# A decoder trunk in which two of the mixer's small matmul groups change places with a projection

## The chip, the cores and the metric

The kernel runs on one NeuronCore of a Trainium2 chip. The metric is the time of one execution on the device, in microseconds; lower is better.

## The reference, cut to what matters

Two layers (DEPTH = 2), each of a half-step SwiGLU, a mixer, a cross attention to a memory, and a second half-step SwiGLU, every one with a residual and a layer norm; 512 positions by 1024 features, float32. The change touches only the mixer:

```
xa, ya, q, k, v, g, lr, c = split_cols(x @ w_in)
# group A, 384 channels in 6 blocks of 64
xc = causal_dwconv(xa, conv_w, conv_b)
r = sigmoid(einsum(xc, w_r) + b_r);  i = sigmoid(einsum(xc, w_i) + b_i)     # recurrent gates
a = exp(-8 * r * softplus(-lam));    h = scan(a, sqrt(1 - a^2) * (i * xc));  out_a = h * gelu(ya)
# group B, 4 heads: gated linear attention in chunks of 64
log_alpha = log_sigmoid(lr @ w_gate + b_gate) / 16                           # linear gates
o = gla_chunked(q, k, v, log_alpha)
o = o * rsqrt(mean(square(o)) + EPS) * norm_g * silu(g)                      # heads' mean squares
# group C, 256 channels in 4 groups of 64
u = causal_dwconv(a_c * sigmoid(gate_c), dw_w, dw_b)                         # 31 taps
out_c = silu((u - mu) * rsqrt(var + EPS) * gn_g + gn_b)                      # group norm
y = concatenate([out_a, out_b, out_c]) @ w_out
```

## The kernel before, in words

Activations lie as features by positions: a tile is 128 features by 512 positions. Each weight and each activation is split into a rounded high part and a low rest, and a product is three passes: high by high, high weight by low activation, low weight by high activation. `tile_of` (line 853) makes one such output tile from 8 feature tiles: 16 passes with the high weights (lines 862 and 865), then 8 with the low ones (line 868), 24 passes in all. `MIX_STEPS` gives each projection of the mixer its PSUM bank and the read that must have freed that bank (`BANK_FREE`).

The weights of a tile are a "slot". Four slots are held as loaded (`raw`), two as split. ScalarE makes the high part of a slot (`w_hi_of`, line 1568) and GpSimd the low part (line 740). `step(layer, s)` in ScalarE's program makes the high part of slot s + 2, after TensorE has finished with slot s. ScalarE's `read(kind, i)` in the mixer is that step followed by the bank, so that every copy out of a projection's bank stands behind making the high weights of the second projection after it. In the mixer the slots come in the order xa 0 to 2, cg 0, ca 0, k 0, k 1, q 0, q 1, cg 1, ca 1, v (two slots), g 0 to 2, ya 0 to 2, then the memory's keys.

The order of the work on each engine is written out by hand; semaphores tie the engines. TensorE's order in the mixer is the list that the change edits. Small matmuls in plain float32 stand between the projections:

- `recurrent_gates(t)`: two 128x512 matmuls (line 1225) for channels tile t, into banks 4 to 7; it waits for the short convolution, and for t = 2 for ScalarE's reads of the first pair.
- `linear_gates()`: two 64-row matmuls (line 1232), into banks 6 and 7; it waits for the copy of k 0 and for the second pair's reads.
- `group_norm(0, SQ, ...)`: one 128x512 matmul (line 1323), the variance of the first group-norm tile.
- `mean_squares()`: three 128x512 matmuls (line 1316) into bank 4, the heads' mean squares.

The profile shows each of these plain float32 matmuls as two records.

ScalarE's order around the first place (lines 1943 to 1978), which the change does not touch:

```
rg_sigmoids(0); rg_sigmoids(1)                       # line 1896, two ACTIVATEs each
A(KK[0], read("k", 0), ACT.Copy)                     # makes q 0's high weights, then copies k 0
rg_sigmoids(2)                                       # waits for the third pair of gates
... 3 Tanh, 3 Exp on the recurrent gates             # lines 1953, 1955
A(KK[1], read("k", 1), ACT.Copy)                     # makes q 1's high weights, then copies k 1
... the linear gates: Abs, Identity, Exp, Ln         # lines 1960 to 1967
A(QQ[0], read("q", 0), ACT.Copy)                     # makes cg 1's high weights, then copies q 0
... 3 Sqrt, decay exponentials; between them read("q", 1)   # makes ca 1's high weights
```

Around the second place ScalarE does: gelu of ya 0, squares of the three head outputs, gelu of ya 1 (behind the step for the first key slot), `group_root(0)` (line 1918, waits for the variance), `head_root()` (line 1908, waits for the mean squares), gelu of ya 2. VectorE's decays (line 2606) wait for the linear gates' logarithm from ScalarE, and its conv taps (line 2585) fill the time between.

Of the kernel before, what the change touches and what calls it, by code (L numbers as in the profile page):

```python
# [163 lines left out]
def raw_norm(layer, n):  # L164
    return layer * len(RAW_NORMS) + RAW_NORMS.index(n)
# [125 lines left out]
def hybrid_decoder(nc, x_in, mem_in, consts_in, vecs_in, mats_in, w_in1, w_out1, w_in2, w_out2,  # L291
                   w_mix, w_v, w_mixout, w_kv, w_q, w_o, out):
    ctx = ExitStack()
    with ctx:
# [85 lines left out]
        def bank(b, rows=P, cols=SEQ):  # L380
            return psum[0:rows, b, 0:cols]
# [30 lines left out]
        def tiles_of(n, count):  # L412
# [37 lines left out]
                                                                 k=KT // 2)  # L450
# [384 lines left out]
        def _(pe):  # L835
# [17 lines left out]
            def tile_of(layer, s, o, operand, n, start=True, stop=True, hi_arrived=None,  # L853
                        lo_arrived=None):
                r = ring(layer, s)
                hi_ready(layer, s)
                for k in range(n):
                    hi = weight(r, k)[0]
                    b_hi, b_lo = operand(k)
                    if hi_arrived:  # L860
                        hi_arrived(k)
                    nc.tensor.matmul(o, hi, b_hi, start=start and k == 0, stop=False)  # L862
                    if lo_arrived:
                        lo_arrived(k)
                    nc.tensor.matmul(o, hi, b_lo, start=False, stop=False)  # L865
                slot_ready(layer, s)
                for k in range(n):
                    last = nc.tensor.matmul(o, weight(r, k)[1], operand(k)[0],  # L868
                                            start=False, stop=stop and k == n - 1)
                last.then_inc(slot_multiplied, 1)  # L870
# [329 lines left out]
            def mixer(layer):  # L1200
                E = layer * EVACS

                def project(kind, i):
                    free = BANK_FREE[kind, i]
                    if free:
                        pe.wait_ge(evac, E + EV[free])
                    if (kind, i) == ("ca", 0):
                        pe.wait_ge(raw_sums_read, 2 * raw_norm(layer, 0) + 2)
                    if (kind, i) == ("ca", 1):
                        pe.wait_ge(xc_ready, layer * AT + AT)  # L1210
                    if (kind, i) == ("k", 0):
                        pe.wait_ge(x_returned, 2 * layer + 1)
                    tile_of(layer, S_MIX + MIX_SLOT[kind, i], bank(MIX_BANK[kind, i]),
                            normed if (kind, i) == ("ca", 0) else act, KT)
# [4 lines left out]
                def recurrent_gates(t):  # L1219
                    pe.wait_ge(xc_ready, layer * AT + t + 1)  # L1220
                    for g in range(2):
                        n = 2 * t + g
                        if n >= 4:
                            pe.wait_ge(rg_gate_read, layer * 6 + n - 3)
                        nc.tensor.matmul(bank(4 + n % 4), mats[:, (AT * g + t) * P:][:, 0:P],
                                         XC[t], start=True, stop=True).then_inc(rg_gate_ready, 1)

                def linear_gates():
                    pe.wait_ge(evac, E + EV["k", 0])
                    pe.wait_ge(rg_gate_read, layer * 6 + 4)  # L1230
                    for g in range(2):
                        last = nc.tensor.matmul(
                            bank(6 + g), mats[0:CHUNK, (2 * AT + g) * P:][:, 0:P],
                            KK[0][0:CHUNK, :], start=True, stop=True)
                    last.then_inc(gla_gate_ready, 1)
# [53 lines left out]
                def output(j):  # L1289

                    if j == 0:
                        pe.wait_ge(state_ready, layer * (NCHUNK - 1) + NCHUNK - 1)
                    for t in range(TT):
                        cols = slice(t * P, (t + 1) * P)
                        for h in range(HEADS):
                            e = h * DV + j * 32
                            nc.tensor.matmul(psum[h * 32:(h + 1) * 32, 5 + j, cols],
                                             v_tok[:, t, e:e + 32], SC[h][:, cols],
                                             start=True, stop=False)
                        for n in (2 * t, 2 * t + 1):  # L1300
                            if n:
                                cols = slice(n * CHUNK, (n + 1) * CHUNK)
                                for h in range(HEADS):
                                    g, r0 = h // 2, h % 2 * CHUNK
                                    last = nc.tensor.matmul(
                                        psum[h * 32:(h + 1) * 32, 5 + j, cols],
                                        state[r0:r0 + CHUNK, n - 1, g, j * 32:(j + 1) * 32],
                                        QQ[g][r0:r0 + CHUNK, cols],
                                        start=False, stop=n % 2 == 1)
                    last.then_inc(o_ready, 1)  # L1310

                def mean_squares():
                    pe.wait_ge(block32_set, 1)
                    for j in range(DVT):
                        pe.wait_ge(o_read, layer * DVT + j + 1)
                        last = nc.tensor.matmul(bank(4), block32[:, :], OSQ[j], start=j == 0,
                                                stop=j == DVT - 1)
                    last.then_inc(rms_ready, 1)

                def group_norm(t, source, ready, signal):  # L1320

                    pe.wait_ge(ready, layer * CT + t + 1)
                    nc.tensor.matmul(bank(CONV_BANK[t]), block64, source[t],
                                     start=True, stop=True).then_inc(signal, 1)
# [18 lines left out]
                recurrent_gates(0)  # L1343
                recurrent_gates(1)
                project("k", 0)
                recurrent_gates(2)
                project("k", 1)
                linear_gates()
                project("q", 0)
                project("q", 1)  # L1350
# [14 lines left out]
                project("ya", 0)  # L1365
                for j in range(DVT):
                    output(j)
                group_norm(0, SQ, gn_squared, gn_var)
                project("ya", 1)
                mean_squares()  # L1370
                project("ya", 2)
                memory_key(0)
# [168 lines left out]
            for layer in range(0, LAYERS):  # L1541
                ffn(layer, 0, 0)
                mixer(layer)
                attention(layer)
                ffn(layer, 1, 3)
# [1396 lines left out]
```

## Time and profile before

| | |
|---|---|
| median of 3 runs | 2122.47 us (2122.47 to 2122.51) |
| profiled execution, its own time | 2121.4 us |
| its span | 2119.6 us |
| TensorE busy | 2099.8 us, 99% |
| VectorE / ScalarE / GpSimd busy | 72% / 51% / 35% |
| mean granted TensorE clock | 0.998 |

The span is what the profile's rows cover; the execution's own time has 1.8 us more around it. "Idle before" in a row is how long that engine had been idle ahead of the row, and the name behind it is what released it. Rows of one kind that touch are merged, with their count behind the x. The mixer runs once in each layer; the stretch that the change touches begins near 385 us and again near 1435 us.

### The profile page before, as it was taken

How to read it: one execution, taken by the hardware profiler on the slowest of the kernel's cores; microseconds unless marked ns; L12 is line 12 of the kernel's file. 1: busy time of each engine (PE TensorE's matmuls, PEld its weight loads, DVE VectorE, ACT ScalarE, POOL GpSimd, SP SyncE). 2: the span in 40 equal slices, each digit the busy share in tenths (PEclk: the TensorE clock that was granted, in tenths of full speed). 3: DMA queues.
4: the chain of work that ended last, by engine and by line, in shares of the span. 5: the costliest groups of instructions: out<-in, count | busy, mean ns of one | idle time of the engine just before them, and what ended most of it. 6: DMA issues, size and time to landing. Idle time of an engine off the chain costs nothing.

```text
span 2119.6 us, 33832 instructions
## 1 busy us (share of the span) xinstructions
PE 2099.8 (99%) x13480; PEld 1882.2 (89%) x13480; DVE 1519.7 (72%) x1965; ACT 1083.5 (51%) x1631; POOL 746.1 (35%) x353
## 2 busy tenths in 40 slices
PE   9999999999999999999999999999999999999997
PEld 7999989788888999998889998897787889999986
DVE  5888535987756998863498884369878479888534
ACT  3666524836344556652366664257364445666422
POOL 4100344536563520024350003445266535100343
PEclk9999999999999999999999999999999999999999
DMA  4555522333332355552245555223243223555531
GB/s 171 139 163 161 185 96 62 90 104 104 113 98 70 106 154 155 165 183 96 77 140 151 159 154 180 92 70 90 90 119 122 88 68 122 150 153 166 172 102 44
DMA packets 118973, 260.99 MB, mean 123 GB/s; under 512 B 41888, under 2 KB 54560, under 8 KB 118560
## 3 DMA queue, kind: packets, MB, share of 16 engines
q1 hardware_dynamic: 109008, 241.95, 35.1%
q0 software_dynamic: 9216, 16.78, 5.3%
q8 instruction: 108, 1.77, 0.3%
q14 instruction: 49, 0.40, 0.1%
q10 hardware_dynamic: 592, 0.08, 0.0%
HBM read 250.38 MB, written 8.39 MB: 122 GB/s over the span
## 4 chain that ended last, share of the span: by engine, by line
PE 95%; ACT 2%; DVE 1%; POOL 1%; issue 0%; DVEq 0%; DMA 0%; ACTq 0%; SPq 0%
PE psum L868 15%; PE psum L862 15%; PE psum L865 15%; PE psum L1059 11%; PE psum L1061 11%; PE psum L1063 11%; PE psum L880 2%; PE psum L1020 1%; PE psum L962 1%; PE psum L1160 1%; PE psum L1159 1%; PE psum L964 1%; PE psum L967 1%; PE psum L886 1%; PE psum L1165 1%; PE psum L837 1%
## 5 line engine op out<-in xcount | busy, mean ns | idle before, releaser
L740 POOL TENSOR_TENSOR w_lo<-raw,w_hi 128x1024 fp32r<-128x1024 f32 (+2 forms) x222 | 611.5, 2758 | 776.6 <-ACT w_hi L1568 755.2
L1568 ACT ACTIVATE w_hi<-raw 128x1024 fp32r<-128x1024 f32 (+2 forms) x222 | 257.3, 1159 | 592.8 <-PE psum L868 514.5
L2398 DVE TENSOR_TENSOR w_lo<-raw,w_hi 128x1024 fp32r<-128x1024 f32 (+2 forms) x204 | 249.9, 1225 | 49.2 <-ACT w_hi L1736 49.1
L1736 ACT ACTIVATE w_hi<-raw 128x1024 fp32r<-128x1024 f32 (+2 forms) x204 | 215.0, 1056 | 108.0 <-PE psum L1063 62.7
L791 POOL DMA_DIRECT2D raw<-w_in x64 | 55.5, 867 | 568.9 <-DMA raw<-w_in 568.8
L862 PE MATMUL psum<-acts_hi,w_hi 128*128 128x512 f32 x632 | 251.2, 397 | 0.0
L865 PE MATMUL psum<-acts_lo,w_hi 128*128 128x512 f32 x632 | 246.2, 390 | 0.0
L865 PE MATMUL psum<-h_lo,w_hi 128*128 128x512 f32 x616 | 239.7, 389 | 0.0
L862 PE MATMUL psum<-h_hi,w_hi 128*128 128x512 f32 x616 | 239.7, 389 | 0.0
L2186 DVE SCALAR_TENSOR_TENSOR x<-x,psum 128x512 f32<-128x512 f32 x54 | 37.0, 685 | 249.3 <-PE psum L868 249.3
L1063 PE MATMUL psum<-acts_hi,w_lo 128*128 128x256 f32 x688 | 194.7, 283 | 0.0
L1061 PE MATMUL psum<-acts_lo,w_hi 128*128 128x256 f32 x688 | 194.7, 283 | 0.0
L1059 PE MATMUL psum<-acts_hi,w_hi 128*128 128x256 f32 x688 | 194.7, 283 | 0.0
L1748 ACT ACTIVATE work<-psum 128x256 f32<-128x256 f32 x272 | 104.4, 384 | 102.6 <-PE psum L1063 96.2
L868 PE MATMUL psum<-acts_hi,w_lo 128*128 128x512 f32 x632 | 156.1, 389 | 0.0
L1059 PE MATMUL psum<-t_in_x,w_hi 128*128 128x256 f32 x544 | 154.4, 284 | 0.0
L1063 PE MATMUL psum<-t_in_x,w_lo 128*128 128x256 f32 x544 | 153.9, 283 | 0.0
L1061 PE MATMUL psum<-t_in_x,w_hi 128*128 128x256 f32 x544 | 153.9, 283 | 0.0
L868 PE MATMUL psum<-h_hi,w_lo 128*128 128x512 f32 x616 | 148.7, 389 | 0.0
L2198 DVE TENSOR_TENSOR work<-work 128x512 f32<-128x512 f32 x52 | 137.3, 2640 | 14.3 <-ACT work L1600 12.5
L862 PEld LDWEIGHTS psum<-acts_hi,w_hi 128*128 128x128 f32 x632 | 118.7, 188 | 28.3 <-issue 3.9
L865 PEld LDWEIGHTS psum<-acts_lo,w_hi 128*128 128x128 f32 x632 | 118.7, 188 | 26.3 <-issue 2.4
(396 smaller groups left out, 5453.2 us busy)
## 6 DMA issues: line engine op xcount, KB each, us to landing
raw<-w_in SPq DMA_DIRECT2D x176, 512.0 KB, 3.6
raw<-w_out SPq DMA_DIRECT2D x64, 704.0 KB, 4.2
raw<-w_in SPq DMA_DIRECT2D x64, 256.0 KB, 3.9
raw<-w_in POOLq DMA_DIRECT2D x64, 256.0 KB, 4.1
raw<-w_kv SPq DMA_DIRECT2D x32, 512.0 KB, 3.4
raw<-w_mix SPq DMA_DIRECT2D x26, 512.0 KB, 3.5
raw<-w_q SPq DMA_DIRECT2D x16, 512.0 KB, 3.4
raw<-w_o SPq DMA_DIRECT2D x16, 512.0 KB, 3.5
```

The source lines that it names most:

```text
L740: nc.gpsimd.tensor_tensor(w_lo[:, n % SPLIT, 0:width], raw[:, n % RAW, 0:width], w_hi[:, n % SPLIT, 0:width].bitcast(F32), ALU.subtract).t ...
L862: nc.tensor.matmul(o, hi, b_hi, start=start and k == 0, stop=False)
L865: nc.tensor.matmul(o, hi, b_lo, start=False, stop=False)
L868: last = nc.tensor.matmul(o, weight(r, k)[1], operand(k)[0], start=False, stop=stop and k == n - 1)
L1059: nc.tensor.matmul(o, hi[:, cols], x_hi[:, k, :], start=start and k == 0, stop=False, skip_group_check=True)
L1061: nc.tensor.matmul(o, hi[:, cols], x_lo[:, k, :], start=False, stop=False, skip_group_check=True)
L1063: last = nc.tensor.matmul(o, lo[:, cols], x_hi[:, k, :], start=False, stop=k == KT // 2 - 1, skip_group_check=True)
L1568: A(w_hi[:, n % SPLIT, 0:width], raw[:, n % RAW, 0:width], ACT.Copy).then_inc(w_hi_made, 1)
L1736: A(o, source, ACT.Copy).then_inc(unit_hi_made, 1)
L1748: A(kept(name), source, ACT.Copy).then_inc(product_kept, 1)
L2198: V.tensor_tensor(zsqsum, zsqsum, zsq(m), ALU.add).then_inc(z_summed, 1)
L2398: V.tensor_tensor(o, source, hi.bitcast(F32), ALU.subtract).then_inc(unit_split, 1)
```

## The change

In both layers, in TensorE's program alone, the third pair of recurrent gates goes from before projection k 1 to behind it, directly ahead of the linear gates; and the first group norm's variance goes from before projection ya 1 to behind it, directly ahead of the mean squares. No operation is added or removed, and no other engine's program is edited.

```
                 recurrent_gates(0)
                 recurrent_gates(1)
                 project("k", 0)
+                project("k", 1)
                 recurrent_gates(2)
-                project("k", 1)
                 linear_gates()
                 project("q", 0)
...
                 for j in range(DVT):
                     output(j)
+                project("ya", 1)
                 group_norm(0, SQ, gn_squared, gn_var)
-                project("ya", 1)
                 mean_squares()
                 project("ya", 2)
```

## Rows read from the trace of the kernel before

**Rows 1.** The page's first part: busy us, share of the span, instructions.
```profile
PE 2099.8 (99%) x13480; PEld 1882.2 (89%) x13480; DVE 1519.7 (72%) x1965; ACT 1083.5 (51%) x1631; POOL 746.1 (35%) x353
```
**Rows 2.** The page's fourth part: the chain that ended last, by engine.
```profile
PE 95%; ACT 2%; DVE 1%; POOL 1%; issue 0%; DVEq 0%; DMA 0%; ACTq 0%; SPq 0%
```
**Rows 3.** Timeline, TensorE, first layer, the gates: start us, us, what, [idle before].
```profile
385.56 3.60 PE L1225 MATMUL psum<-tmp,mats 128*128 128x512 f32 x8
...
394.46 1.88 PE L1225 MATMUL psum<-tmp,mats 128*128 128x512 f32 x4
...
403.66 0.50 PE L862 MATMUL psum<-acts_hi,w_hi 128*128 128x512 f32 x1
404.00 0.40 PE L865 MATMUL psum<-acts_lo,w_hi 128*128 128x512 f32 x1
```
**Rows 4.** Timeline, TensorE, first passes of q 1, cg 1 and ca 1.
```profile
409.23 0.39 PE L862 MATMUL psum<-acts_hi,w_hi 128*128 128x512 f32 x1
...
414.67 0.39 PE L862 MATMUL psum<-acts_hi,w_hi 128*128 128x512 f32 x1
...
420.11 0.39 PE L862 MATMUL psum<-acts_hi,w_hi 128*128 128x512 f32 x1
```
**Rows 5.** Timeline, ScalarE, first layer, from the second pair's sigmoids to v.
```profile
389.20 0.69 ACT L1896 ACTIVATE tmp<-psum,vecs 128x512 f32<-128x512 f32 x1 [0.17 <-PE psum L1225]
394.66 1.06 ACT L1568 ACTIVATE w_hi<-raw 128x1024 fp32r<-128x1024 f32 x1 [4.77 <-PE psum L868]
...
396.10 1.26 ACT L1896 ACTIVATE tmp<-psum,vecs 128x512 f32<-128x512 f32 x2
...
402.55 1.04 ACT L1568 ACTIVATE w_hi<-raw 128x1024 fp32r<-128x1024 f32 x1
403.50 0.58 ACT L1956 ACTIVATE tmp<-psum 128x512 f32<-128x512 f32 x1
...
410.94 0.58 ACT L1968 ACTIVATE tmp<-psum 128x512 f32<-128x512 f32 x1
...
418.26 1.08 ACT L1568 ACTIVATE w_hi<-raw 128x1024 fp32r<-128x1024 f32 x1
...
425.75 1.49 ACT L1568 ACTIVATE w_hi<-raw 128x1536 fp32r<-128x1536 f32 x1 [2.04 <-PE psum L868]
```
**Rows 6.** ScalarE in one stretch: us, busy us, instructions, clock, DMA share, GB/s.
```profile
401.50:419.90 18.40, 18.21 (x28) 1.00 0.32 78
```
**Rows 7.** Timeline, VectorE: first decay, and the second mask with idle before it.
```profile
409.94 0.69 DVE L2606 SCALAR_TENSOR_TENSOR psum<-psum,tmp 128x512 f32<-128x512 f32 x1
...
456.68 1.37 DVE L2640 COPY_PREDICATED work<-consts,psum 128x1024 f32<-128x1024 uint32 x1 [2.71 <-PE psum L1264]
```
**Rows 8.** Timelines, memory keys: ScalarE's high weights and the TensorE pass they release.
```profile
509.62 1.04 ACT L1568 ACTIVATE w_hi<-raw 128x1024 fp32r<-128x1024 f32 x1
...
510.81 0.35 PE L862 MATMUL psum<-mem_hi,w_hi 128*128 128x256 f32 x1 [0.83 <-ACT w_hi L1568]
```
**Rows 9.** Timelines, second layer: ca 1's high weights and its first pass.
```profile
1468.52 1.08 ACT L1568 ACTIVATE w_hi<-raw 128x1024 fp32r<-128x1024 f32 x1
...
1470.38 0.39 PE L862 MATMUL psum<-acts_hi,w_hi 128*128 128x512 f32 x1
```
**Rows 10.** Timelines, second place: TensorE's variance and mean squares, ScalarE's two roots.
```profile
479.26 1.13 PE L1323 MATMUL psum<-tmp,consts 128*128 128x512 f32 x2
...
485.68 2.74 PE L1316 MATMUL psum<-tmp,block 128*128 128x512 f32 x6
...
488.74 0.69 ACT L1918 ACTIVATE tmp<-psum,small 128x512 f32<-128x512 f32 x1
...
490.03 0.67 ACT L1908 ACTIVATE tmp<-psum,small 128x512 f32<-128x512 f32 x1
```
**Rows 11.** End of the span: us, busy us and count of PE, PEld, DVE, ACT, POOL, clock.
```profile
2100.00:2110.00 10.00, 7.92 (x58) 7.06 (x56) 7.70 (x15) 3.95 (x10) 0.49 (x1) 1.00 0.15 54
2110.00:2119.00 9.00, 0.00 (x0) 0.00 (x0) 6.02 (x12) 4.48 (x9) 4.33 (x5) 0.63 0.50 176
```

More of the change, by code:

```diff
@@ L1345, in mixer @@
                 project("k", 0)
+                project("k", 1)
                 recurrent_gates(2)
-                project("k", 1)
                 linear_gates()
@@ L1367, in mixer @@
                     output(j)
+                project("ya", 1)
                 group_norm(0, SQ, gn_squared, gn_var)
-                project("ya", 1)
                 mean_squares()
```

## The prediction

> **What bounds the kernel now.** I read the page's busy shares first. TensorE is busy 99% of the span, ScalarE about half [rows 1], and the chain that ended last lies on TensorE for 95% [rows 2]. So a small gain can only come from fewer or cheaper TensorE records, and the change has the same records. A loss, though, can come from anything that makes TensorE wait, and that is to be looked for in the engines' orders, not in the shares. The second view is therefore the timeline of TensorE and of ScalarE side by side at the two places. The reader is to see that between the third pair's sigmoids (396.10) and the high weights of ca 1 (418.26) ScalarE stands still nowhere worth naming: in 401.50 to 419.90 it is busy 18.21 of 18.40 us [rows 5, 6]. Here ScalarE is nearly as tight as TensorE, though its share over the span is 51%.
>
> **First place: the third pair behind k 1.** A projection takes 5.44 us, the distance of the first passes of q 1, cg 1 and ca 1 [rows 4] (24 passes of 0.227). On TensorE the swap changes little. The four records of the pair cost about 0.43 each (8 records of the first two pairs in 3.60, the last of them 0.59 long [rows 3]) wherever they stand. What joining them to the linear gates can save is between nothing and all that they cost over ordinary passes, 4 x (0.43 - 0.227) = 0.8 us in a layer; a loss has a reason only if the linear gates' change to 64 rows costs more behind slow records than behind quick ones, and I bound that by the same 0.8. I take 0: whatever it is, it lies ahead of the waits below, which swallow it.
>
> ScalarE's order isn't edited, and it works strictly down its list, as the front part shows: the third pair's sigmoids, three Tanh, three Exp, then q 1's high weights and the copy of k 1. The swap gives it the third pair one projection later. The sum:
> - TensorE's row of the pair begins at 394.46 + 5.44 = 399.90 and ends 1.88 later, 401.78 [rows 3].
> - For the second pair the row ended at 385.56 + 3.60 = 389.16 and the last sigmoid began at 389.20, 0.04 later, and took 0.69 [rows 3, 5]. So the third pair's last sigmoid ends at 401.78 + 0.04 + 0.69 = 402.51.
> - Before, the two ended at 396.10 + 1.26 = 397.36 [rows 5]. ScalarE is 5.15 us late. Ahead of the pair it just idles.
> - Behind it nothing gives the time back until it next waits for TensorE, which is at 425.75, with 2.04 idle [rows 5].
>
> Queued behind the late sigmoids, each by 5.15 us, are what TensorE waits for:
> - q 1: k 1's copy (it frees the bank) ends at 403.50 + 0.58 + 5.15 = 409.23. A pass starts 0.15 after ScalarE ends (509.62 + 1.04 = 510.66, pass at 510.81) [rows 8]. So q 1 starts at 409.38 where it stood at 409.23 [rows 4, 5]. After such a wait the second pass comes 0.34 behind the first (403.66, 404.00 [rows 3]) where 0.227 is usual, 0.11 more. About 0.26 late.
> - cg 1: q 0's copy ends at 410.94 + 0.58 + 5.15 = 416.67, the pass starts at 416.82 where it stood at 414.67: with the 0.11, 2.26 late in all, so a new wait of about 2.0.
> - ca 1: its high weights end at 418.26 + 1.08 + 5.15 = 424.49, the first pass starts at 424.64 where it stood at 420.11: 4.53 + 0.11 = 4.64 late in all, a second wait of about 2.4.
>
> The last of them sets the cost: 4.64 us. The high weights of ca 1 had been 0.77 ahead of their pass, and 5.15 - 0.77 + 0.15 + 0.11 is the same number. Next is v, whose high weights for the second slot wait for TensorE itself, with 2.04 idle before them: from there ScalarE follows TensorE again.
>
> VectorE: its first decay starts at 409.94 [rows 7] behind the linear gates' logarithms, which now come 5.15 later, so it is at most 5.15 late, 0.5 more than TensorE. It has 2.71 idle before the second mask, where it waits for TensorE; I count nothing. GpSimd makes ca 1's low weights from the high ones; TensorE wants them 16 passes, 3.6 us, after its first. Counted as nothing; if both engines' contention for it gave half a microsecond, it would still be covered. The weights' DMAs are issued in an order that stays, and TensorE being late only makes them earlier.
>
> Second layer: ca 1's high weights end at 1469.60 and its pass stands at 1470.38, 0.78 apart [rows 9], against 0.77. Same cost. Together 2 x 4.64 = 9.3 us.
>
> **Second place: the variance behind ya 1.** It takes two records from 479.26 and puts them ahead of the six from 485.68 [rows 10]. The eight still end at 485.68 + 2.74 = 488.42, and ya 1 ends some 0.86 us sooner. ScalarE's first root (488.74) follows gelu of ya 1 and so could start at 487.88; the variance is there by about 484.82 + 1.13 = 485.95. Its second root (490.03) could start at 489.17, 0.75 behind the mean squares. So neither wait bites. What the join saves is between 0 and the excess of two records, 0.4 us in a layer, what it could lose no more; without a row for it I take 0, the nearest, since all eight stay slow. If the cover were gone, the 1.9 us of the first root would be the margin.
>
> **Sum.** Profiled execution 2121.4 + 9.3 = 2130.7. The median of the runs, 2122.47, stands 1.07 above that execution; I put the same 9.3 on it: 2131.7 us. The span would be 2128.9.
>
> **The clock.** The granted clock was 1.00 in 2100 to 2110, with TensorE idle for 2.08 of it, and 0.63 on average in 2110 to 2119, in which TensorE did nothing more [rows 11]. The new waits, 2.0 and 2.4 us, are shorter than that tail, about the size of the idle time that left the clock alone. The Trainium skill ("TensorE: Matmul & The Clock Gate", "HAM oscillation — how this bites in real kernels") has it that an array left idle for long enough falls to half its clock and starts its next work cold; by it two long waits close together are what to be afraid of here. It makes no term of the sum and stands among the rivals.
>
> **Rivals.**
> - *No change.* ScalarE has idle time elsewhere (4.77 before 394.66, 2.04 before 425.75), and 51% says slack. If the delay were taken up before ca 1, the time would be 2122.4, within a few tenths for the saved transitions (at best 2 x (0.8 + 0.4) = 2.4 less, 2120.1). It decides for this case if the delay is under 0.6 us (0.77 less the hand-over). Against it: the idle stretches lie ahead of the late sigmoids and behind ca 1; none between. 6%.
> - *More than this.* A clock drop after the long waits. At 1.2 GHz in place of 2.4 the tile behind it takes up to 5.44 more; once in a layer gives 2131.7 + 10.9 = 2142.6. For it: two waits of over 2 us within 8. Against it: rows 11's first. 4%.
> - *Part of it.* The last wait is smaller, because something in ScalarE's chain that I count as work is itself waiting and shrinks when late. All of what isn't busy in the stretch is 0.19 us in 18.40 [rows 6], so little is there; half of the delay gone would be 2127.1. 4%.
>
> **The numbers.** My forecast 85%, faster by over 0.2% 1%. What a measurement of this kernel can tell from no change is about 0.2%, 4.2 us. Slower by over that needs the forecast or the two last rivals: 0.93; within it 0.06. Range 2128.5 to 2134.0: downwards 1.6 us a layer for savings and a hand-over that I took wrong, upwards some 1.2 a layer for VectorE's half microsecond and GpSimd's.
>
> **What would show it.** In the profile after: the third pair's sigmoids at about 401 to 402.5 with ScalarE idle before them; a TensorE wait released by ScalarE ahead of q 1 (small), cg 1 (about 2.0) and ca 1 (about 2.4), in both layers; v some 4.6 later; the first layer's end later by that and no more; the roots of the second place where they are relative to ya 1. I am wrong if ScalarE's line from Tanh to ca 1 shortens, if ca 1 stands less than 4 us or more than 5.5 later, or if the granted clock falls under 1 in the mixer.

## The result: 9.2 us slower, and the profile after

The changed kernel took 2131.74 us in the median of 6 runs (2131.29 to 2132.24), the kernel before 2122.49 (2122.47 to 2122.67, 6 runs): ratio 1.0045, 95% interval 1.0033 to 1.0056. Forecast was 2131.7, range 2128.5 to 2134.0.

The shares of the page of the profile say nothing of it. Its first part after, against [rows 1]:
```profile
PE 2102.8 (99%) x13480; PEld 1882.7 (88%) x13480; DVE 1520.0 (71%) x1965; ACT 1083.1 (51%) x1631; POOL 744.0 (35%) x353
```
The waits of TensorE over the whole execution say most of it (engine and line, released by what: us in total, times, longest):
```profile
PE psum L862 <- ACT w_hi L1568: 6.0, 4, 2.2
PE psum L862 <- ACT tmp L1968: 3.3, 2, 1.7
```
Before, the first of these was 1.7 us in 2 waits and the second was not there, so 4.3 + 3.3 = 7.6 us of waiting are new. The rest of the loss does not show as idle time: a pass that had to wait starts later than the row's idle time says, by the end of the pass before it (modelled ends overlap the next start by some 0.16 us), and the pass behind it follows 0.1 later than usual.

ScalarE's timeline after, in the first layer, which answers to [rows 5] (start us, us, what, idle before). All of this execution is 0.88 us late here already, before its first pair of gates:
```profile
390.08 0.69 ACT L1896 ACTIVATE tmp<-psum,vecs 128x512 f32<-128x512 f32 x1 [0.17 <-PE psum L1225]
395.53 1.06 ACT L1568 ACTIVATE w_hi<-raw 128x1024 fp32r<-128x1024 f32 x1 [4.76 <-PE psum L868]
...
401.84 0.69 ACT L1896 ACTIVATE tmp<-psum,vecs 128x512 f32<-128x512 f32 x1 [4.77 <-PE psum L1225]
402.70 0.69 ACT L1896 ACTIVATE tmp<-psum,vecs 128x512 f32<-128x512 f32 x1 [0.17 <-PE psum L1225]
...
416.95 0.57 ACT L1968 ACTIVATE tmp<-psum 128x512 f32<-128x512 f32 x1
...
424.27 1.08 ACT L1568 ACTIVATE w_hi<-raw 128x1024 fp32r<-128x1024 f32 x1
```
The reader is to see the new 4.77 us of idle time ahead of the third pair's sigmoids, which is ScalarE waiting for TensorE, and no idle time printed between them and ca 1's high weights (424.27). TensorE after, in the first layer, against [rows 3, 4]:
```profile
386.44 3.60 PE L1225 MATMUL psum<-tmp,mats 128*128 128x512 f32 x8
...
400.78 1.88 PE L1225 MATMUL psum<-tmp,mats 128*128 128x512 f32 x4
402.59 1.98 PE L1232 MATMUL psum<-tmp,mats 64*128 64x512 f32 x4
...
410.15 0.50 PE L862 MATMUL psum<-acts_hi,w_hi 128*128 128x512 f32 x1
...
417.58 0.50 PE L862 MATMUL psum<-acts_hi,w_hi 128*128 128x512 f32 x1 [1.65 <-ACT tmp L1968]
...
425.49 0.47 PE L862 MATMUL psum<-acts_hi,w_hi 128*128 128x512 f32 x1 [2.13 <-ACT w_hi L1568]
```
These are q 1, cg 1 and ca 1, each the first pass behind ScalarE's late work.

The table sets each kernel's TensorE records against the same records of the kernel before: how much later a record starts, in us. Every experiment below is read from it, since it separates the two layers and shows by itself, in its first column, what differs from one execution to the next at the start. From left to right: the first pair of gates in layer 1, then q 1, cg 1, ca 1 and v there, the end of the mixer there, the first pair of gates in layer 2, cg 1 and v there, the last matmul of all. For q 1, cg 1 and ca 1 the record is one a few passes behind the first, so that the slow first pass after a wait is in it. What a layer costs is v less the column at which the layer begins.

| profiled execution of | before 1st pair | q 1 | cg 1 | ca 1 | v | 1st mixer's end | before 2nd | cg 1 | v | last matmul |
|---|---|---|---|---|---|---|---|---|---|---|
| changed | 0.88 | 1.06 | 3.03 | 5.47 | 5.49 | 5.50 | 5.49 | 7.65 | 10.11 | 10.01 |
| e1 first edit only | 1.31 | 1.49 | 3.44 | 5.89 | 5.92 | 5.91 | 5.82 | 8.00 | 10.41 | 10.37 |
| e2 second edit only | 1.02 | 1.02 | 1.02 | 1.02 | 1.02 | 0.99 | 0.99 | 0.99 | 0.99 | 0.91 |
| e3 ScalarE late | 1.13 | 1.58 | 3.55 | 6.00 | 7.66 | 7.63 | 7.60 | 10.06 | 12.52 | 12.43 |
| e5 one Tanh more | 0.00 | 0.00 | 0.00 | 0.23 | 0.26 | 0.23 | 0.45 | 0.45 | 0.68 | 0.57 |
| e6 k 1 first | 0.00 | -0.05 | 1.00 | 3.45 | 3.48 | 3.44 | 3.34 | 4.35 | 8.42 | 8.29 |
| e7 k 1 and q 1 first | 1.31 | 1.27 | 2.31 | 2.33 | 2.33 | 2.29 | 2.25 | 3.26 | 3.26 | 3.25 |
| e4 repaired | 1.45 | 1.40 | 1.40 | 1.40 | 1.97 | 7.95 | 7.86 | 7.82 | 8.41 | 13.37 |
| e9 repaired, taps moved | 1.65 | 1.60 | 1.60 | 1.60 | 2.19 | 2.15 | 2.08 | 2.03 | 2.59 | 2.50 |

In the changed kernel a layer costs 5.49 - 0.88 = 4.61 and 10.11 - 5.49 = 4.62.

The second place after, against [rows 10] (TensorE, then ScalarE):
```profile
490.33 1.02 PE L1323 MATMUL psum<-tmp,consts 128*128 128x512 f32 x2
491.19 2.74 PE L1316 MATMUL psum<-tmp,block 128*128 128x512 f32 x6
```
```profile
493.38 0.69 ACT L1918 ACTIVATE tmp<-psum,small 128x512 f32<-128x512 f32 x1
494.14 0.63 ACT L1920 ACTIVATE tmp<-tmp 128x512 f32<-128x512 f32 x1
494.68 0.67 ACT L1908 ACTIVATE tmp<-psum,small 128x512 f32<-128x512 f32 x1
```
Less the 5.50 of this stretch the mean squares stand at 485.69 (485.68 before) and the roots (lines 1918 and 1908) at 487.88 and 489.18, 0.86 and 0.85 sooner than before: ya 1 ended that much sooner, and no root waits.

### The profile page after: what moved, and what is told of

Same layout as the page of the kernel before. It is cut to its first block, busy times and chain, and to the rows that moved or that the text cites. A ratio compares the mean times of both kernels' runs of the same rounds, so it can differ in the third digit from the quotient of the medians.

```text
span 2129.5 us, 33832 instructions
## 1 busy us (share of the span) xinstructions
PE 2102.8 (99%) x13480; PEld 1882.7 (88%) x13480; DVE 1520.0 (71%) x1965; ACT 1083.1 (51%) x1631; POOL 744.0 (35%) x353
## 4 chain that ended last, share of the span: by engine, by line
PE 93%; ACT 3%; DVE 1%; POOL 1%; issue 1%; DVEq 0%; ACTq 0%; DMA 0%; SPq 0%
PE psum L868 14%; PE psum L862 14%; PE psum L865 14%; PE psum L1059 11%; PE psum L1061 11%; PE psum L1063 11%; PE psum L880 2%; PE psum L1020 1%; PE psum L962 1%; PE psum L1160 1%; PE psum L1159 1%; PE psum L964 1%; PE psum L967 1%; PE psum L886 1%; PE psum L1165 1%; ACT w_hi L1568 1%
```

## The experiments

My theory: the first edit makes ScalarE get its third pair late, its list runs strictly in order, and TensorE waits for what stands behind. The rivals: TensorE itself pays for the joined slow records; the second edit shares in it; VectorE, late as well, sets the end. In the changed kernel's own profile the new waits of TensorE all have ScalarE as their releaser; its waits for VectorE in the mixer are as they were (one of 0.3 us in a layer).

**e1, the first edit alone.**
```
                 project("k", 0)
+                project("k", 1)
                 recurrent_gates(2)
-                project("k", 1)
```


> Only the first edit: the third pair of recurrent gates behind k 1; the variance stays ahead of ya 1. Theory (ScalarE in order): this edit carries all of the loss, 4.62 us a layer in the trace of the changed kernel, so 2131.7 us, with new TensorE waits of 1.7 and 2.1 us ahead of cg 1 and ca 1. Rival (the loss is shared with the second edit, by the eight slow records joined or by the later root): under 2130.

Measured: 2131.54 us (2130.14 to 2133.17) against 2122.12 for the kernel before on that chip, ratio 1.0046 (1.0033 to 1.006). That is all of the loss, to within the interval, and in the table a layer costs 5.92 - 1.31 = 4.61 and 10.41 - 5.82 = 4.59, as in the changed kernel.

**e2, the second edit alone.**
```
+                project("ya", 1)
                 group_norm(0, SQ, gn_squared, gn_var)
-                project("ya", 1)
```


> Only the second edit: the variance behind ya 1, beside the mean squares. Theory: no wait bites, the join of slow records saves at most hundredths: 2122.4 to 2122.5 us, v and everything before as in the kernel before. Rival (the later variance holds up ScalarE's root and what follows): 2123 or more, with ScalarE idle before its line of the first root.

Measured: 2121.92 against 2122.12, ratio 0.9999 (0.999 to 1.0008). In the table its row stays flat. ya 1 itself runs 0.86 sooner (0.16 late where what is around it is 1.02 late), and behind the mean squares all of that but 0.03 is given back. Joining the variance to the mean squares is worth 0.02 to 0.03 us in this layer and nothing that the table shows in the other.

**e3, ScalarE late by other means, TensorE's order as before.** This is the experiment that separates ScalarE's lateness from where the gates stand.
```
                 for t in range(AT):
                     A(TH[t], RR[t], ACT.Tanh, scale=l(11)[:, t:t + 1])
+                for n in range(8):
+                    if n % AT == 0:
+                        act.drain()
+                    A(TH[n % AT], RR[n % AT], ACT.Tanh, scale=l(11)[:, n % AT:n % AT + 1])
```


> The kernel before, with TensorE's order as it was; ScalarE repeats 8 of its Tanh instructions (with 3 drains) behind the third pair's sigmoids, same results. At 0.62 us each that makes it 4.9 to 5.5 us late there. Theory (ScalarE being late is enough by itself): a delay d costs TensorE d - 0.77 + 0.15 + 0.11 a layer, 4.4 to 5.0, so 2131.3 to 2132.5 us, with waits ahead of cg 1 and ca 1 as in the changed kernel. Rival (what costs is TensorE's own order, the third pair beside the 64-row matmuls): 2122.5, or at most what is seen with VectorE, under 2125.

Measured: 2133.64 (2132.4 to 2133.81), ratio 1.0055 (1.0041 to 1.0068). The added Tanh group, and the waits on TensorE:
```profile
398.56 1.95 ACT L1953 ACTIVATE tmp<-tmp,lam 128x512 f32<-128x512 f32 x3
400.58 5.37 ACT L1957 ACTIVATE tmp<-tmp,lam 128x512 f32<-128x512 f32 x8
405.96 1.28 ACT L1959 ACT_TABLE_LOAD   x1
```
```profile
418.11 0.50 PE L862 MATMUL psum<-acts_hi,w_hi 128*128 128x512 f32 x1 [1.69 <-ACT tmp L1972]
421.87 1.98 PE L868 MATMUL psum<-acts_hi,w_lo 128*128 128x512 f32 x8
426.02 0.47 PE L862 MATMUL psum<-acts_hi,w_hi 128*128 128x512 f32 x1 [2.18 <-ACT w_hi L1568]
```
ScalarE is d = 405.96 - (398.56 + 1.95) = 5.45 late; the prediction's formula, d - 0.77 + 0.15 + 0.11 = d - 0.51, gives 4.94, and the second layer shows 12.52 - 7.60 = 4.92. So ScalarE's lateness alone, with no gate moved, gives the same waits at the same two places. The median is 1.1 above the expected 2131.3 to 2132.5. What goes beyond the expectation is in the first layer, where v is 7.66 - 6.00 = 1.66 later than ca 1. TensorE's clock fell there; the stretches (us, busy and count of PE, PEld, DVE, ACT, POOL, clock, DMA share, GB/s):
```profile
420.00:425.00 5.00, 3.85 (x17) 2.84 (x16) 4.74 (x8) 4.97 (x10) 0.04 (x1) 1.00 0.65 103
425.00:430.00 5.00, 3.98 (x12) 3.20 (x13) 4.96 (x3) 4.97 (x6) 4.04 (x2) 0.74 0.04 6
430.00:435.00 5.00, 5.00 (x24) 4.34 (x24) 5.00 (x5) 1.66 (x2) 2.38 (x2) 0.92 0.88 137
```
In the second layer, behind waits of 1.67 and 2.18 us, it was 1.00.

**e5, the lead.** As e3 with one Tanh and one drain instead of eight.

> The kernel before with one Tanh repeated behind the third pair's sigmoids (with one drain), same results; ScalarE is some 0.7 to 0.8 us late there in place of 5.15. Theory (TensorE is held by ScalarE only by what exceeds the lead of ca 1's high weights, 0.62 us): TensorE loses 0.1 to 0.3 us a layer, 2122.3 to 2122.8. Rival (each microsecond on ScalarE costs one on TensorE, no lead): 1.5 us more than before.

Measured: 2123.03 against 2122.27, ratio 1.0004 (0.9994 to 1.0013). The median is 0.2 above the expected 2122.3 to 2122.8 and 0.8 below the rival's 2123.8, and the interval takes in no change at all, so the runs alone settle little; the table does. A layer costs 0.26 and 0.23 us. The rows give the dose:
```profile
397.43 1.95 ACT L1953 ACTIVATE tmp<-tmp,lam 128x512 f32<-128x512 f32 x3
399.45 0.72 ACT L1957 ACTIVATE tmp<-tmp,lam 128x512 f32<-128x512 f32 x1
400.18 1.28 ACT L1959 ACT_TABLE_LOAD   x1
```
400.18 - (397.43 + 1.95) = 0.80 late, for which the formula has 0.80 - 0.51 = 0.29. Most of the first 0.80 us costs nothing, and the 4.65 more that e3 adds are paid in full (4.92 - 0.23 = 4.69): TensorE is held by what exceeds the lead, which is how long before its pass ca 1's high weights used to be ready.

**e4, ScalarE's list mended on the changed kernel.**
```
+                A(KK[1], read("k", 1), ACT.Copy).then_inc(evac, 1)
                 rg_sigmoids(2)
...
-                A(KK[1], read("k", 1), ACT.Copy).then_inc(evac, 1)
...
+                A(QQ[0], read("q", 0), ACT.Copy).then_inc(evac, 1)
                 for g in range(2):
                     A(CU[g], CU[g], ACT.Ln, bias=1.0).then_inc(gla_log, 1)
-                A(QQ[0], read("q", 0), ACT.Copy).then_inc(evac, 1)
+                A(QQ[1], read("q", 1), ACT.Copy).then_inc(evac, 1)
...
                     if g:
-                        A(QQ[1], read("q", 1), ACT.Copy).then_inc(evac, 1)
+                        step(layer, S_MIX + MIX_SLOT["cg", 1])
...
-                A(CC[1], read("cg", 1), ACT.Sigmoid).then_inc(evac, 1)
+                A(CC[1], bank(MIX_BANK["cg", 1]), ACT.Sigmoid).then_inc(evac, 1)
```


> The changed kernel, both edits, with ScalarE's order changed and nothing added: the step and copy of k 1 go ahead of the third pair's sigmoids, the step and copy of q 0 ahead of the linear gates' Ln, the step and copy of q 1 right behind that Ln, the step of cg 1 between the two groups of decay exponentials. Theory: the third pair is late as before, but nothing that TensorE waits for stands behind it, so the waits ahead of q 1, cg 1 and ca 1 go and the time is 2122.3 to 2123.0 us. Rival (the join itself costs on TensorE, or VectorE's delay does): 2127 or more.

Measured: 2134.29 (2133.66 to 2134.82), ratio 1.0058 (1.0043 to 1.0073): slower than the changed kernel, and far from the expected 2122.3 to 2123.0. The waits for ScalarE did go (q 1, cg 1 and ca 1 all at 1.40, where the layer began at 1.45). Another came. VectorE's timeline, then TensorE's second scores, then the clock:
```profile
416.68 0.70 DVE L2607 SCALAR_TENSOR_TENSOR psum<-psum,tmp 128x512 f32<-128x512 f32 x1 [5.22 <-ACT tmp L1968]
...
459.55 1.34 DVE L2641 COPY_PREDICATED tmp<-consts,psum 128x1024 f32<-128x1024 uint32 x1
```
```profile
460.95 2.08 PE L1264 MATMUL psum<-tmp 64*128 64x128 f32 x16 [3.44 <-DVE tmp L2641]
```
```profile
455.00:460.00 5.00, 2.51 (x12) 1.73 (x10) 4.70 (x7) 1.54 (x2) 1.32 (x1) 0.96 0.82 336
460.00:465.00 5.00, 4.05 (x35) 3.41 (x36) 2.64 (x4) 0.00 (x0) 1.03 (x1) 0.50 0.37 108
465.00:470.00 5.00, 5.00 (x21) 4.05 (x20) 0.54 (x2) 0.00 (x0) 0.00 (x0) 0.86 0.00 0
```
VectorE's decays need the linear gates' logarithm from ScalarE, which is still late, and behind them stands the mask for which TensorE's second scores wait. In the changed kernel that lateness was covered by TensorE being 4.6 late itself. There the mask began at 458.31 and the second scores at 460.95, so the mask was done 1.3 us ahead:
```profile
458.31 1.35 DVE L2640 COPY_PREDICATED tmp<-consts,psum 128x1024 f32<-128x1024 uint32 x1
```
```profile
460.95 1.16 PE L1264 MATMUL psum<-tmp 64*128 64x128 f32 x16
```
With TensorE on time, it waits 3.4 us there, and behind this long wait the clock was at 0.50 for a stretch: 7.95 - 1.97 = 5.98 us are lost between v and the mixer's end in the first layer, of which the wait is 3.4. The second layer has the same: a wait of 3.40, the clock at 0.77 and 0.89 in the two stretches of 5 us around and behind it, and 13.37 - 8.41 = 4.96 lost behind v.

**e9, e4 with VectorE's taps moved.** If that is so, VectorE has to have something to do while it waits.
```
-                taps(0, 0, 24)
+                taps(0, 0, 30)
                 for g in range(2):
                     decays(g)
...
-                taps(0, 24, CONV_K)
+                taps(0, 30, CONV_K)
```


> The repaired kernel (2134.3) with one thing more: VectorE does 30 of the first conv tile's 31 taps ahead of its decays in place of 24, filling the 5.2 us for which it waited for the linear gates' logarithm, so nothing behind the decays is late by more than some 0.5 us. Theory (in the repaired kernel VectorE's lateness, 3.4 us of wait at the second scores and the clock fall behind it, was the whole loss, ScalarE's waits being gone): both go, what stays is 0.35 to 0.6 a layer ahead of v, 2123.0 to 2123.6, granted clock 1.00 throughout the mixer. Rival (the loss there had to do with the joined gates or with GpSimd's two slots in a row): 2128 or more.

Measured: 2123.69 (2123.0 to 2123.95), 0.1 above what was expected, ratio 1.0008 (0.9999 to 1.0018). The changed TensorE order, both edits in it, and only 1.42 us above the kernel before on that chip (2122.27), where the changed kernel had 9.25. The interval takes in no change. In the table 2.50 - 1.65 = 0.85 of it lies behind the first pairs of gates. VectorE's wait ahead of the decays, and the one wait of TensorE that is left in this stretch:
```profile
416.88 0.70 DVE L2607 SCALAR_TENSOR_TENSOR psum<-psum,tmp 128x512 f32<-128x512 f32 x1 [0.24 <-ACT tmp L1968]
```
```profile
427.67 0.41 PE L880 MATMUL psum<-w_hi,acts_hi 128*128 128x384 f32 x1 [0.35 <-ACT tmp L1978]
```
TensorE's second scores wait no more, and the clock was at 1.00 there (455 to 475). What is left, 0.59 and 0.56 us ahead of v, is the last piece of ScalarE's lateness; whether another order of its list could take that up too was not tried. TensorE's own part is a gain: 0.05 from the pairs to q 1 in each layer.

**e6, k 1 first only**, the first hunk of e4 on the changed kernel.

> The changed kernel with ScalarE's step and copy of k 1 ahead of the third pair's sigmoids, nothing else. ScalarE is then late by about 4.0 us instead of 5.15 from the linear gates on (from the ScalarE timeline of the repaired kernel: first Abs 1.1 us sooner than in the changed one). Theory: no wait ahead of q 1, about 1.0 ahead of cg 1, ca 1 late by 4.0 - 0.51 = 3.5 us a layer: 2129.1. VectorE's mask keeps its lead, since TensorE is late too. Rival (VectorE sets the end as in the repaired kernel): 2133 or more.

Measured: 2130.17 (2129.61 to 2130.94), ratio 1.0039 (1.0024 to 1.0054). The first layer is as forecast: 1.00 at cg 1, 3.45 at ca 1, VectorE no part. The waits ahead of these were 0.77 and 2.18 us, in both layers. Yet in the second v is at 8.42, 5.08 more than the layer began with, where the first lost 3.48, and the clock fell again behind them:
```profile
1475.00:1480.00 5.00, 2.93 (x8) 2.32 (x9) 4.93 (x5) 4.98 (x8) 3.00 (x2) 0.78 0.17 27
```
The difference is 1.6 us, and it may be why the median is 1.1 above the expectation; there are no rows for the other timed runs, so that is not shown.

**e7, e6 with q 1's and cg 1's steps as in e4**, q 0's copy left behind the Ln.

> As the last, and q 1's step and copy right behind q 0's, cg 1's step between the two groups of decay exponentials. Theory with two paths: by ScalarE TensorE is late by 1.1 us at cg 1 and no more at ca 1 and v; VectorE's decays are 3.7 late, its first mask had a lead of 1.73 us over TensorE's second scores, so a new wait of 3.7 - 1.1 - 1.73, about 0.9, appears there: 2.0 a layer, 2126.2 in all, with no fall of the clock. Rival (ScalarE is the only path): 2124.4, no wait for the mask.

Measured: 2124.38 (2123.24 to 2124.61), ratio 1.001 (1.0001 to 1.002). One wait is left, 0.77 ahead of cg 1: a layer costs 2.33 - 1.31 = 1.02 and 3.26 - 2.25 = 1.01. That is the rival's 2124.4 and not the 2126.2 of my theory, which was wrong in its second path: the decays were late (idle time of 3.55 us), yet the mask was late by too little to hold TensorE.
```profile
414.90 0.70 DVE L2607 SCALAR_TENSOR_TENSOR psum<-psum,tmp 128x512 f32<-128x512 f32 x1 [3.55 <-ACT tmp L1967]
...
455.88 1.34 DVE L2641 COPY_PREDICATED tmp<-consts,psum 128x1024 f32<-128x1024 uint32 x1
```
Less 1.31 for the start, the decays are 414.90 - 1.31 - 409.94 = 3.65 late, but the mask is at 454.57, where it was at 452.62: 1.95 late and not 3.7. VectorE's instructions with all operands in SBUF have two prices here: 0.68 us, and up to 4.0 when they ran beside GpSimd's splitting of weights (line 740). Two neighbours of VectorE's in e7, and GpSimd's row; the first had begun before GpSimd did:
```profile
426.44 0.68 DVE L2623 TENSOR_TENSOR tmp<-tmp 128x512 f32<-128x512 f32 x1
427.05 4.00 DVE L2621 SCALAR_TENSOR_TENSOR tmp<-tmp 128x512 f32<-128x512 f32 x1
```
```profile
426.57 7.83 POOL L740 TENSOR_TENSOR w_lo<-raw,w_hi 128x1536 fp32r<-128x1536 f32 x2 [5.39 <-ACT w_hi L1568]
```
Between the decays and the mask the long ones cost 10.8 us over their short price in the kernel before (records of 2.83, 3.99, 4.00 and 3.26) and 9.1 in e7 (0.99, 4.00, 3.99 and 2.88). The 1.7 between them is the 3.65 - 1.95 that VectorE got back. So its lateness shrinks or not with what it collides with, and a sum of durations over such a stretch is good to a microsecond or two only.

## Why the prediction was right

- *The pair's sigmoids 5.15 late.* Measured 402.70 + 0.69 - 0.88 = 402.51, the forecast to the hundredth, against 397.36 before.
- *Nothing behind them gives it back before 425.75.* Right, from the timeline (behind the late sigmoids ScalarE first waits for TensorE again at v's second slot, at 431.24 with 1.59 us idle), and e3 and e5 show by the dose that it is this that counts.
- *q 1 about 0.26 late, cg 1 2.26, ca 1 4.64.* Measured from 0.88: 0.18, 2.15, 4.59. The waits as rows show them are 1.65 and 2.13 where I had 2.0 and 2.4: what I gave was lateness, of which the idle time in a row is less by the end of the pass before. One term was too large: I took 0.15 us from ScalarE's end to the pass for every hand-over. Behind ca 1's high weights it was 425.49 - (424.27 + 1.08) = 0.14, but behind q 0's copy 417.58 - (416.95 + 0.57) = 0.06. That is most of the 0.11 by which cg 1 came sooner than forecast, and it costs nothing, since ca 1 sets the end.
- *The join on TensorE at 0.* It is worth 0.05 us a layer at the first place (e9, q 1 against the pairs) and 0.03 at most at the second. As I had put it, ScalarE's waits swallow the first: ca 1 is not sooner for it.
- *VectorE at nothing.* Right in effect, but for the wrong reason, and so in part by luck: its 2.71 us of idle time before the second mask was the wrong row to name. TensorE's second scores wait for the first mask, which ended at 453.96, 1.5 before their records in the kernel before:
```profile
452.62 1.34 DVE L2640 COPY_PREDICATED tmp<-consts,psum 128x1024 f32<-128x1024 uint32 x1
...
455.47 1.16 PE L1264 MATMUL psum<-tmp 64*128 64x128 f32 x16
```
  The forecast needed half a microsecond of that lead, and it was there; e4, in which TensorE is no longer late with VectorE, needed more than there was.
- *The second place at 0, root margins 1.9 and 0.75.* Right (e2).
- *The sum.* 9.3 forecast, 9.25 measured between the medians. In the profiled executions the span grew by 9.9; 0.88 of that was there before the first pairs, and the same column reads 0.00 to 1.65 in the others, so it belongs to the execution and not to the change.
- *The clock rival, 4%.* Not in the changed kernel's profile, yet e3's waits, of the same lengths, brought it in one of two layers, and e6's of 0.77 and 2.18 us too. It cost some 1.6 us each time in them, and beyond the wait itself 2.5 and 1.6 in e4's two layers, not 5.4. I had its price too high, and what I set against it was weak: the 2.08 us without TensorE in [rows 11] were not one wait, the longest being this one.
```profile
2108.25 0.70 PE L1020 MATMUL psum<-x,consts 128*128 128x256 f32 x2 [1.48 <-DVE x L2222]
```
  A wait of 1.48 us that left the clock alone says nothing of waits of 2.0 and more, so my likelihood was probably too low as well; that the changed kernel's profiled execution kept its clock behind 2.13 and 2.18 us is in part luck.

## What to carry to other kernels

When a small operation is moved later on the busiest engine, look at who consumes it and at what stands behind that consumer's instruction in its own list; an engine at 51% over the span can be without a gap just there. The cost is the lateness less the smallest lead among the things behind it that the busy engine needs (here not q 1, the first of them, but ca 1, the last), and each lead is read from two rows. When such a lateness is mended on one engine, look at the next one that got it: here VectorE became the bound, hidden until then only by the stall that was removed.

## What the runs showed of the hardware that I had not expected

The granted clock of TensorE fell behind waits of 1.69 and 2.18 us some 8 apart in e3's first layer (0.74 over 5 us, 1.66 us lost) and not in its second, nor in either layer of the changed kernel and of e1, whose waits were of 1.64 to 1.69 and 2.13 to 2.18. In e6, with 0.77 and 2.18, it fell in the second layer alone. So it fell in 2 of the 8 places that have such a wait of 2.1 to 2.2 us, and whether the shorter wait ahead of it has a part was not tested. Behind one wait of 3.4 us in e4 it was at 0.50, the 1.2 GHz level, for a whole stretch of 5 us. The Trainium skill ("TensorE: Matmul & The Clock Gate", "HAM oscillation — how this bites in real kernels") ties the fall to one idle gap that is long enough. e4 agrees with that: 3.4 us, then 0.50. e3 and e6 show a fall behind shorter gaps too, and with the same gaps no fall; what decides between the two was not settled.

VectorE's plain 128x512 instructions in SBUF took 0.68 us or up to 4.0 us, the long ones only while GpSimd was splitting weights (rows under e7), while those with an operand in PSUM stayed at 0.67 to 0.76 beside the same work. It is how a lateness of 3.65 us at e7's decays became 1.95 at the mask.
